# Differential attention: half of the weights-times-values products in split fp32r, and three quarters of the joining of the two maps on GpSimd

## The chip, the cores and the metric

The kernel runs on one core of one Trainium2 chip, in one launch. The metric is the device time in microseconds. Three runs of the kernel before took 2998.64, 2998.72 and 3003.08 us, median 2998.72. The profile shown here is of one further execution.

## The reference, cut to what matters

A two-layer encoder is applied to a prompt of 2048 tokens and a sample of 256 tokens with shared weights. The first layer mixes by differential attention, the second by a Fourier transform. The attention, per head (8 heads, two query/key maps of 64, values of 128):

```python
def block(start):
    qb = lax.dynamic_slice_in_dim(q, start, Q_BLOCK, axis=3)          # 128 queries, both maps
    s = jnp.einsum('bhmqd,bhmkd->bhmqk', qb, k, preferred_element_type=f32) * scale
    s = s - (slopes[:, None, None] * dist)[None, :, None]             # ALiBi
    p = jax.nn.softmax(s, axis=-1)
    pd = p[:, :, 0] - lam * p[:, :, 1]                                # the two maps are joined
    return jnp.einsum('bhqk,bhkv->bhqv', pd.astype(v.dtype), v)       # weights times values
```

Everything is float32.

## The kernel before, in words

The function `attend` does all heads in one program without a loop on the chip. A head has 17 steps: step q from 0 to 15 handles the scores of the q-th block of 128 prompt queries, and step 16 those of the sample. The work on one block is spread over several steps. In the terms of the code:

- **Scores.** Step q computes four halves (`score_half`, j = 0 to 3: map 0 keys 0 to 1023, map 0 keys 1024 to 2047, then map 1), each into one of three PSUM buffers of 1024 columns (`score`, RING = 3). VectorE takes the row maximum of each half (`maximum`, L1296) and scales it (`negative`, L1302). ScalarE takes the exponential of each half (`exponential`, L1220) with its row sums. A half can be written only when the exponential three halves earlier is done.
- **Joining.** In the next step VectorE adds the row sums and inverts them (`inverse_sums`, L1320, L1323; this runs behind the step's first row maximum), and p0/sum0 - lambda * p1/sum1 is formed in place: GpSimd scales the first half of map 1 (L1388, 1024 keys), then the second half of map 1 (L1391) and of map 0 (L1393), and adds these two (L1396). VectorE does the first half of the keys with one scalar_tensor_tensor (`combine`, L1334), the last thing in its step.
- **Turning.** One step later, TensorE transposes the joined block in four units of four key blocks (`turn_weights`, c = 0 to 3, L1096) into one single PSUM buffer `turned` of 512 columns; ScalarE copies each unit to SBUF (`take_weights`, L1198). The next unit must wait for that copy. In steps 1 to 5 a unit of the values is transposed too (`turn_value`, L1105, copied by `take_v`, L1204, which stands between the third and the fourth exponential on ScalarE).
- **Products.** `pair_product` (L1122, and L1116 for the sample) multiplies 16 key blocks by a pair of query blocks, 256 columns, into `o_acc`. The table `QUARTERS` deals 130 products to the quarters of the steps; in steps 5 to 14 each quarter has two.

All five engines run in the order in which their code is written. TensorE's order in a usual step is: half 0, half 1, turn 0, pair 0, turn 1, half 2, pair 1, turn 2, half 3, turn 3, pair 2, turn_value (steps 1 to 5), pair 3. VectorE's is: maximum 0, inverse_sums, maximum 1, negative 0, maximum 2, maximum 3, negative 1, combine. In the profile one fp32 product or fp32 matmul of the program shows as two MATMUL records, an fp32r one as one.

## Time and profile before

| | us |
|---|---|
| median of three runs | 2998.72 |
| the profiled execution | 3001.8 |
| its span, first to last instruction | 2999.7 |
| TensorE busy in the span | 2834.2 (94%) |
| VectorE | 1831.8 (61%) |
| ScalarE | 1740.7 (58%) |
| GpSimd | 1637.9 (55%) |
| attention stage, about 852 to 2081 | 1229 |

The time of a run is some 2 us more than the span. Matmul durations in the timeline include their pipeline, so the pitch of matmuls is read from the difference of their starts.

### The profile page before, as it was taken

The numbers are of one execution on the slowest core, as the hardware profiler recorded it, in microseconds if no ns is written. First come the engines' busy times: TensorE is split into PE (matmuls) and PEld (weight loads), VectorE is DVE, ScalarE is ACT, GpSimd is POOL, SyncE is SP. The second block draws the span as 40 slices with busy tenths as digits, with TensorE's granted clock in tenths as the row PEclk, the third lists the DMA queues.
The fourth block names the chain that finished last, engine by engine and source line by source line (L and its number), as shares of the span: only waits on it lengthen the run. The fifth ranks groups of instructions, "written<-read, shape, count | busy, mean of one in ns | idle before, by whom it ended". The sixth has DMA issues, their size and how long they took to land. (4 is left out here: it accounts for less than half of the span.)

```text
span 2999.7 us, 41691 instructions
## 1 busy us (share of the span) xinstructions
PE 2834.2 (94%) x15098; PEld 2493.8 (83%) x15098; DVE 1831.8 (61%) x2402; ACT 1740.7 (58%) x3126; POOL 1637.9 (55%) x1060
## 2 busy tenths in 40 slices
PE   3899999999899999999999999998999899899898
PEld 3899999999778787878888888886688899887687
DVE  7668767866476777777777777776886200441322
ACT  4777766776477777777777777775443321322321
POOL 5888764654266566656665666665664320230642
PEclk8999999999999999999999999999999999999899
DMA  2654464356344413141313232121565522555752
GB/s 84 197 173 166 146 198 127 118 181 201 101 130 138 107 34 102 35 108 36 98 46 76 65 74 64 37 90 60 199 207 172 187 90 77 158 168 186 263 186 102
DMA packets 281816, 374.03 MB, mean 125 GB/s; under 512 B 22923, under 2 KB 258507, under 8 KB 276140
## 3 DMA queue, kind: packets, MB, share of 16 engines
q1 hardware_dynamic: 279404, 369.14, 39.6%
q8 instruction: 121, 1.98, 0.3%
q10 hardware_dynamic: 2080, 2.10, 0.2%
q14 instruction: 83, 0.68, 0.1%
q0 software_dynamic: 128, 0.13, 0.0%
HBM read 258.04 MB, written 125.97 MB: 128 GB/s over the span
## 5 line engine op out<-in xcount | busy, mean ns | idle before, releaser
L1296 DVE TENSOR_REDUCE pa_half_max<-pa_score 128x1 f32<-128x1024 f32 x512 | 624.2, 1219 | 324.9 <-PE pa_score L1066 324.4
L1220 ACT ACTIVATE pa_p<-pa_score,pa_neg_max 128x1024 f32<-128x1024 f32 x512 | 567.7, 1111 | 68.6 <-DVE pa_neg_max L1302 68.4
L206 PE MATMUL ia_acc<-ia_xh,ia_wh 128*128 128x384 f32 x1344 | 459.9, 342 | 73.3 <-DVE ia_xl L686 44.1
L1122 PE MATMUL pa_o_acc<-pa_wt,pa_vv 128*128 128x256 f32 x2048 | 514.0, 380 | 1.5 <-ACT pa_o_out_s L1259 1.5
L1062 PE MATMUL pa_score<-pa_ka,pa_qa 128*128 128x512 f32 x1024 | 454.9, 444 | 13.2 <-ACT pa_p L1220 6.6
L207 PE MATMUL ia_acc<-ia_xl,ia_wh 128*128 128x384 f32 x1344 | 456.2, 339 | 0.0
L208 PE MATMUL ia_acc<-ia_xh,ia_wl 128*128 128x384 f32 x1344 | 455.8, 339 | 0.0
L1198 ACT ACTIVATE pa_wt<-pa_turned 128x512 f32<-128x512 f32 x512 | 306.3, 598 | 241.4 <-PE pa_turned L1096 236.4
L443 POOL TENSOR_TENSOR ia_w_sums<-ia_raw 128x512 f32<-128x512 f32 x240 | 334.3, 1401 | 174.3 <-PE ia_acc L208 158.8
L1066 PE MATMUL pa_score<-pa_kb,pa_qb 96*128 96x512 f32 x1024 | 422.9, 413 | 0.0
L1122 PEld LDWEIGHTS pa_o_acc<-pa_wt,pa_vv 128*128 128x128 f32 x2048 | 366.2, 190 | 44.8 <-ACT pa_o_out_s L1259 3.2
L1388 POOL TENSOR_SCALAR pa_p<-pa_p,pa_inv_sum,pa_lam_neg 128x1024 f32<-128x1024 f32 x128 | 153.6, 1200 | 447.8 <-DVE pa_inv_sum L1323 447.8
L206 PEld LDWEIGHTS ia_acc<-ia_xh,ia_wh 128*128 128x128 f32 x1344 | 258.2, 192 | 79.8 <-issue 79.4
L1096 PE MATMUL pa_turned<-pa_ident,pa_p 128*128 128x128 f32 x2048 | 313.0, 275 | 3.9 <-ACT pa_wt L1198 3.6
L1396 POOL TENSOR_TENSOR pa_p<-pa_p 128x1024 f32<-128x1024 f32 x128 | 302.4, 2363 | 23.8 <-POOL pa_p L1393 23.8
L1096 PEld LDWEIGHTS pa_turned<-pa_ident,pa_p 128*128 128x128 f32 x2048 | 243.1, 140 | 77.8 <-ACT pa_wt L1198 39.5
L670 DVE TENSOR_TENSOR ia_wl<-ia_acc,ia_wh 128x512 fp32r<-128x512 f32 x336 | 227.1, 683 | 84.4 <-ACT ia_acc L569 83.3
L706 DVE TENSOR_TENSOR ia_c<-ia_c,ia_acc 128x384 f32<-128x384 f32 x384 | 198.3, 547 | 126.2 <-PE ia_acc L208 116.6
L207 PEld LDWEIGHTS ia_acc<-ia_xl,ia_wh 128*128 128x128 f32 x1344 | 258.3, 192 | 0.5
L208 PEld LDWEIGHTS ia_acc<-ia_xh,ia_wl 128*128 128x128 f32 x1344 | 257.8, 192 | 0.0
L1062 PEld LDWEIGHTS pa_score<-pa_ka,pa_qa 128*128 128x128 f32 x1024 | 196.4, 192 | 53.1 <-ACT pa_p L1220 13.7
L1066 PEld LDWEIGHTS pa_score<-pa_kb,pa_qb 96*128 96x128 f32 x1024 | 196.9, 192 | 33.6
...
## 6 DMA issues: line engine op xcount, KB each, us to landing
...
```

The source lines that it names most:

```text
L206: pe.matmul(out, a_hi(k), b_hi(k), start=first and n == 0, stop=False)
L207: pe.matmul(out, a_hi(k), b_lo(k), start=False, stop=False)
L208: mm = pe.matmul(out, a_lo(k), b_hi(k), start=False, stop=last and n == len(ks) - 1)
L443: pool.tensor_tensor(w_sums[:, s % RING], x, y, op).then_inc(w_sum, 1)
L1062: pe.matmul(out[:, c], qa[s][:, n, at:at + P], ka[hs][:, n, cols], start=True, stop=False)
L1066: mm = pe.matmul(out[:, c], qb[s][:, n, at:at + P], kb[hs][n][:, cols], start=False, stop=True)
L1096: mm = pe.transpose(turned[:, x * P:(x + 1) * P], src, ident[:])
L1122: mm = pe.matmul(acc, vv[:, k], wt[:, g % 2, k], start=k == 0, stop=k == NB - 1)
L1198: act.activation(wt[:, s, 4 * c:4 * c + 4, at:at + P], turned[:].rearrange("p (k t) -> p k t", k=4), ACT.Copy).then_inc(turned_out, 1)
L1220: act.activation(dst[:, half * HALF:(half + 1) * HALF], score[:, (4 * q + j) % RING].rearrange("p a b -> p (a b)"), ACT.Exp, bias=neg_max[ ...
L1296: dve.tensor_reduce(half_max[:, q % 2, n, half:half + 1], score[:, (4 * q + j) % RING].rearrange("p a b -> p (a b)"), AX_X, ALU.max).then_ ...
L1396: pool.tensor_tensor(b, b, p1[:, par, HALF:], ALU.add).then_inc(weights_rest, 1)
```

## The change

Key blocks 4 to 7 and 12 to 15 (units c = 1 and 3, `LOW`) are kept as two fp32r numbers, a rounded one and the remainder, for the weights (`wt_hi`, `wt_lo`) and the values (`vv_hi`, `vv_lo`). Their product is three fp32r matmuls of 256 columns in place of one fp32 one. ScalarE's copy writes the rounded part; VectorE writes the remainder, PSUM minus rounded part (`weights_low`, L1379 of the changed kernel, and `v_low`, L1385), after which `turned` may be overwritten: every turn waits for the semaphore `low_out` as well. `weights_low` for c = 1 stands between negative 0 and maximum 2; for c = 3 it stands behind combine, and `v_low` behind that (steps 2 and 4). On TensorE `turn_value` moves behind pair 3. GpSimd's part of the joining grows from 1024 to 1536 of 2048 keys, and VectorE's combine shrinks from 1024 to 512; turn 1 waits for GpSimd's part, before it was turn 2, and the third exponential does, before the fourth. To make room, some small tiles share memory and the sample uses the diagonal table of the last pair (one DMA a head less).

```diff
@@ attend: buffers @@
+    LOW = (1, 3)
+    LOW_NB = 4 * len(LOW)
...
-        vv = m.sb("vv", [P, NB + 2, P])
+        vv = m.sb("vv", [P, NB + 2 - LOW_NB, P])
+        vv_hi = m.sb("vv_hi", [P, LOW_NB, P], F32R)
+        vv_lo = m.sb("vv_lo", [P, LOW_NB, P], F32R)
...
-        wt = m.sb("wt", [P, 2, NB, PAIR])
+        wt = m.sb("wt", [P, 2, NB - LOW_NB, PAIR])
+        wt_hi = m.sb("wt_hi", [P, 2, LOW_NB, PAIR], F32R)
+        wt_lo = m.sb("wt_lo", [P, 2, LOW_NB, PAIR], F32R)
...
@@ TensorE: turn_weights, turn_v, pair_product, step @@
-                    if c == 2:
+                    if c == 1:
                         pe.wait_ge(weights_rest, NB * h + t - 1 if t >= 2 else NB * h)
                     wait(pe, turned_out, unit(h, t, "w", c))
+                    wait(pe, low_out, lows(h, t, "w", c))
...
                     wait(pe, turned_out, unit(h, t, "v", c))
+                    wait(pe, low_out, lows(h, t, "v", c))
...
+                                if c in LOW:
+                                    pe.wait_ge(low_out, lows(h, t, kind, c) + 1 - (LOWS if late else 0))
+                            if is_low(k):
+                                at = low_at(k)
+                                pe.matmul(acc, vv_hi[:, at], wt_hi[:, g % 2, at], start=False, stop=False)
+                                pe.matmul(acc, vv_hi[:, at], wt_lo[:, g % 2, at], start=False, stop=False)
+                                mm = pe.matmul(acc, vv_lo[:, at], wt_hi[:, g % 2, at], start=False, stop=k == NB - 1)
...
                         pair(2)
+                        pair(3)
                         turn_value(q - 1)
-                        pair(3)
@@ ScalarE: take_weights, take_v, exponential @@
+                    dst = wt_hi[:, s, low_at(4 * c):low_at(4 * c) + 4, at:at + P] if c in LOW else \
+                        wt[:, s, full_at(4 * c):full_at(4 * c) + 4, at:at + P]
...
-                    if j == 3 and not (is_first(h) and q < 2):
+                    if j == 2 and not (is_first(h) and q < 2):
                         act.wait_ge(weights_rest, NB * h + (q - 1 if q >= 1 else -1))
@@ VectorE: combine, new weights_low and v_low, step @@
-                    a, par = p0[:, (q - 1) % 4, :HALF], (q - 1) % 2
-                    dve.scalar_tensor_tensor(out=a, in0=a, scalar=inv_sum[:, par, 0:1], in1=p1[:, par, :HALF],
+                    a, par = p0[:, (q - 1) % 4, :GROUP], (q - 1) % 2
+                    dve.scalar_tensor_tensor(out=a, in0=a, scalar=inv_sum[:, par, 0:1], in1=p1[:, par, :GROUP],
                                              op0=ALU.mult, op1=ALU.add).then_inc(weights, 1)
+
+                def weights_low(h, t, c):
+                    dve.wait_ge(turned_out, unit(h, t, "w", c) + 1)
...
+                    dve.tensor_tensor(wt_lo[:, s, ks, at:at + P], turned[:].rearrange("p (k t) -> p k t", k=4),
+                                      f32(wt_hi[:, s, ks, at:at + P]), ALU.subtract).then_inc(low_out, 1)
...
                             negative(h, q, 0)
+                        low(1)
+                        if parts["score"]:
                             maximum(h, q, 2)
                             maximum(h, q, 3)
                             negative(h, q, 1)
                     if parts["before"]:
                         combine(h, q)
+                    low(3)
+                    if parts["score"] and (q, "v", q - 1) in place and q - 1 in LOW:
+                        v_low(h, q, q - 1)
@@ GpSimd @@
-                    pool.tensor_scalar(p1[:, par, :HALF], p1[:, par, :HALF], inv_sum[:, par, 1:2], lam["neg"][:, 0:1],
+                    pool.tensor_scalar(p1[:, par, :GROUP], p1[:, par, :GROUP], inv_sum[:, par, 1:2], lam["neg"][:, 0:1],
                                        ALU.mult, ALU.mult).then_inc(p1_scaled, 1)
-                    b = p0[:, (q - 1) % 4, HALF:]
+                    b = p0[:, (q - 1) % 4, GROUP:]
...
-                    pool.tensor_tensor(b, b, p1[:, par, HALF:], ALU.add).then_inc(weights_rest, 1)
+                    pool.tensor_tensor(b, b, p1[:, par, GROUP:], ALU.add).then_inc(weights_rest, 1)

```

How VectorE's order changes, first before. From the reciprocal of one step to that of the next (pa_half_max: a row maximum; pa_p: the combine):

```order
L1320 TENSOR_TENSOR pa_row_sum<-pa_half_sum 128x2
L1323 RECIPROCAL pa_inv_sum<-pa_row_sum 128x2
L1296 TENSOR_REDUCE pa_half_max<-pa_score 128x1
L1302 TENSOR_SCALAR pa_neg_max<-pa_half_max 128x1
L1296 TENSOR_REDUCE pa_half_max<-pa_score 128x1 x2
L1302 TENSOR_SCALAR pa_neg_max<-pa_half_max 128x1
L1334 SCALAR_TENSOR_TENSOR pa_p<-pa_p,pa_inv_sum 128x1024
L1296 TENSOR_REDUCE pa_half_max<-pa_score 128x1
```

and now, in step 4 of a head:

```order
L1357 TENSOR_TENSOR pa_row_sum<-pa_half_sum 128x2
L1360 RECIPROCAL pa_inv_sum<-pa_row_sum 128x2
L1333 TENSOR_REDUCE pa_half_max<-pa_score 128x1
L1339 TENSOR_SCALAR pa_neg_max<-pa_half_max 128x1
L1379 TENSOR_TENSOR pa_wt_lo<-pa_turned,pa_wt_hi 128x4x128
L1333 TENSOR_REDUCE pa_half_max<-pa_score 128x1 x2
L1339 TENSOR_SCALAR pa_neg_max<-pa_half_max 128x1
L1371 SCALAR_TENSOR_TENSOR pa_p<-pa_p,pa_inv_sum 128x512
L1379 TENSOR_TENSOR pa_wt_lo<-pa_turned,pa_wt_hi 128x4x128
L1385 TENSOR_TENSOR pa_vv_lo<-pa_turned,pa_vv_hi 128x512
L1333 TENSOR_REDUCE pa_half_max<-pa_score 128x1
```

Two remainders of the weights and one of the values have come in, two of the three directly behind the combine and ahead of the next step's first row maximum.

TensorE at the end of step 4, before (L1096 is turn 3, L1105 turn_value, L1062 the first matmul of step 5):

```order
L1096 MATMUL pa_turned<-pa_ident,pa_p 128x128 x4
L1122 MATMUL pa_o_acc<-pa_wt,pa_vv 128x256
L1105 MATMUL pa_turned<-pa_ident,pa_vt 128x128 x4
L1122 MATMUL pa_o_acc<-pa_wt,pa_vv 128x256
L1062 MATMUL pa_score<-pa_ka,pa_qa_51 128x512
```

and now (L1123, L1133 and L1088 in their place):

```order
L1123 MATMUL pa_turned<-pa_ident,pa_p 128x128 x4
L1154 MATMUL pa_o_acc<-pa_wt_hi,pa_vv_hi 128x256
L1155 MATMUL pa_o_acc<-pa_wt_lo,pa_vv_hi 128x256
L1156 MATMUL pa_o_acc<-pa_wt_hi,pa_vv_lo 128x256
L1154 MATMUL pa_o_acc<-pa_wt_hi,pa_vv_hi 128x256
L1155 MATMUL pa_o_acc<-pa_wt_lo,pa_vv_hi 128x256
L1156 MATMUL pa_o_acc<-pa_wt_hi,pa_vv_lo 128x256
L1133 MATMUL pa_turned<-pa_ident,pa_vt 128x128 x4
L1088 MATMUL pa_score<-pa_ka,pa_qa_51 128x512
```

Each of the two products has become three matmuls, and the values are turned behind both. 

GpSimd keeps its order of four instructions a step; three of them, two TENSOR_SCALAR and the TENSOR_TENSOR, have 1536 columns where they had 1024, and the first TENSOR_SCALAR 512.

## Rows read from the trace of the kernel before

**Rows 1.** Windows: stretch, length, busy us of each engine (instructions), clock, DMA.

```profile
852.00:2081.00 1229.00, 1211.10 (x6583) 1007.39 (x6582) 887.42 (x1181) 909.03 (x1680) 764.65 (x519) 1.00 0.26 73
1401.70:1410.90 9.20, 9.20 (x52) 7.76 (x51) 6.77 (x10) 6.78 (x13) 5.92 (x4) 1.00 0.02 5
```

**Rows 2.** Waits inside the attention stage: us in total, times, longest.

```profile
PEld pa_turned L1096 <- ACT pa_wt L1198: 37.6, 173, 1.0
PEld pa_turned L1105 <- ACT pa_wt L1198: 24.2, 30, 1.1
```

**Rows 3.** Timeline of TensorE, one step: start us, us, what, count.

```profile
1403.86 0.60 PE L1096 MATMUL pa_turned<-pa_ident,pa_p 128*128 128x128 f32 x4
1404.30 1.03 PE L1122 MATMUL pa_o_acc<-pa_wt,pa_vv 128*128 128x256 f32 x4
1405.16 0.64 PE L1096 MATMUL pa_turned<-pa_ident,pa_p 128*128 128x128 f32 x4
...
1409.37 1.89 PE L1122 MATMUL pa_o_acc<-pa_wt,pa_vv 128*128 128x256 f32 x8
1410.91 0.58 PE L1062 MATMUL pa_score<-pa_ka,pa_qa 128*128 128x512 f32 x1
```

**Rows 4.** TensorE timeline, fp32r products of 260 columns, Fourier layer.

```profile
2576.26 0.28 PE L207 MATMUL fl_ps<-fl_wc,fl_ring 128*128 128x260 f32 x1
...
2577.94 0.28 PE L206 MATMUL fl_ps<-fl_wc,fl_ring 128*128 128x260 f32 x1
```

**Rows 5.** Timeline of ScalarE, same step as rows 3.

```profile
1404.50 0.60 ACT L1198 ACTIVATE pa_wt<-pa_turned 128x512 f32<-128x512 f32 x1 [0.75 <-PE pa_turned L1096]
```

**Rows 6.** Timeline of VectorE, same step.

```profile
1404.35 0.17 DVE L1323 RECIPROCAL pa_inv_sum<-pa_row_sum 128x2 f32<-128x2 f32 x1
...
1410.53 1.40 DVE L1334 SCALAR_TENSOR_TENSOR pa_p<-pa_p,pa_inv_sum 128x1024 f32<-128x1024 f32 x1
1412.23 1.22 DVE L1296 TENSOR_REDUCE pa_half_max<-pa_score 128x1 f32<-128x1024 f32 x1 [0.30 <-PE pa_score L1066]
```

**Rows 7.** Timeline of GpSimd, same step.

```profile
1404.73 1.21 POOL L1388 TENSOR_SCALAR pa_p<-pa_p,pa_inv_sum,pa_lam_neg 128x1024 f32<-128x1024 f32 x1 [3.09 <-DVE pa_inv_sum L1323]
...
1408.48 2.36 POOL L1396 TENSOR_TENSOR pa_p<-pa_p 128x1024 f32<-128x1024 f32 x1 [0.18 <-POOL pa_p L1393]
```

**Rows 8.** Timeline of GpSimd, a step with a long overlap.

```profile
1452.97 2.36 POOL L1396 TENSOR_TENSOR pa_p<-pa_p 128x1024 f32<-128x1024 f32 x1 [0.18 <-POOL pa_p L1393]
```

**Rows 9.** Timeline of VectorE, that step.

```profile
1454.31 2.10 DVE L1334 SCALAR_TENSOR_TENSOR pa_p<-pa_p,pa_inv_sum 128x1024 f32<-128x1024 f32 x1
```

**Rows 10.** Line 1334, all executions: ns shortest/median/longest.

```profile
L1334 DVE SCALAR_TENSOR_TENSOR pa_p<-pa_p,pa_inv_sum x128: 1275/1391/2956, 831.5 to 2057.3; 128x1024 f32<-128x1024 f32 x128
```

**Rows 11.** Groups of GpSimd: busy us, mean ns of one.

```profile
L1388 POOL TENSOR_SCALAR pa_p<-pa_p,pa_inv_sum,pa_lam_neg 128x1024 f32<-128x1024 f32 x128 | 153.6, 1200 | 447.8 <-DVE pa_inv_sum L1323 447.8
...
L2005 POOL TENSOR_TENSOR fg_xl<-fg_h_in,fg_xh 128x1536 fp32r<-128x1536 f32 x10 | 35.1, 3515 | 108.0 <-ACT fg_xh L2038 108.0
...
L1383 POOL TENSOR_SCALAR pa_p_s<-pa_p_s,pa_inv_s,pa_lam_neg 128x256 f32<-128x256 f32 x16 | 8.8, 559 | 4.7 <-DVE pa_inv_s L1316 4.7
```

**Rows 12.** Groups of VectorE: a difference of PSUM and SBUF; the row maximum.

```profile
L1296 DVE TENSOR_REDUCE pa_half_max<-pa_score 128x1 f32<-128x1024 f32 x512 | 624.2, 1219 | 324.9 <-PE pa_score L1066 324.4
L670 DVE TENSOR_TENSOR ia_wl<-ia_acc,ia_wh 128x512 fp32r<-128x512 f32 x336 | 227.1, 683 | 84.4 <-ACT ia_acc L569 83.3
```

**Rows 13.** Timeline of VectorE, reciprocals of steps 1 and 6.

```profile
1448.85 0.17 DVE L1323 RECIPROCAL pa_inv_sum<-pa_row_sum 128x2 f32<-128x2 f32 x1
...
1495.65 0.17 DVE L1323 RECIPROCAL pa_inv_sum<-pa_row_sum 128x2 f32<-128x2 f32 x1
```

**Rows 14.** Line 1316, once a head: first and last start.

```profile
L1316 DVE RECIPROCAL pa_inv_s<-pa_sum_s x8: 166/168/178, 972.0 to 2061.3; 128x4 f32<-128x4 f32 x8
```

**Rows 15.** Windows around an idle stretch of TensorE, columns as in rows 1.

```profile
2114.80:2117.40 2.60, 0.03 (x1) 0.00 (x1) 2.56 (x3) 1.06 (x1) 1.12 (x1) 1.00 0.09 32
2117.50:2121.00 3.50, 3.50 (x5) 1.47 (x6) 3.50 (x2) 1.07 (x2) 2.27 (x2) 0.53 0.00 0
```

More of the change, by code:

```diff
@@ L835, in attend @@
         qb_s = m.sb("qb_s", [HD + ALIBI, 2, SHORT], F32R)
-        diag_s = m.sb("diag_s", [P, P], F32R)
+        p_s_at = (nc.sbuf_base + 31) // 32 * 32
         p_s = m.sb("p_s", [P, 2, 2, SHORT])
-        wt_s = m.sb("wt_s", [P, 2, SHORT])
+        wt_s = p_s[:, 1]
         o_out_s = m.sb("o_out_s", [P, SHORT])
@@ L845, in attend @@
         ones = m.sb("ones", [P, P])
-        sq = m.sb("sq", [P, 2, 2, GROUP])
-        row_w = m.sb("row_w", [P, 1])
-        eps = m.sb("eps", [P, 1])
+        small = m.sb("small", [P, 3])
+        row_w, eps = small[:, 0:1], small[:, 1:2]
         score = m.ps("score", [P, RING, 2, GROUP])
@@ L878, in attend @@
         pool_held, sp_held = m.sem("pool_held"), m.sem("sp_held")
-        lam = load_lambda(m, m.sem("lam_in"))
+        lam = load_lambda(m, m.sem("lam_in"), p_s_at, small[:, 2:3])
         order = []
@@ L892, in unit, with lows, is_low, full_at @@
             return UNITS * h + place[(t, kind, c)] - SKIPPED
+        low_order = [x for x in order if x[2] in LOW]
+        LOWS = len(low_order)
+        SKIPPED_LOWS = len(LOW)
+        def lows(h, t, kind, c):
+            return LOWS * h + sum(place[x] < place[(t, kind, c)] for x in low_order) - SKIPPED_LOWS
+        def is_low(k):
+            return k // 4 in LOW
+        def full_at(k):
+            return sum(not is_low(x) for x in range(k))
+        def low_at(k):
+            return sum(is_low(x) for x in range(k))
         def turned_block(t):
@@ L979, in load_sample @@
                         sp.dma_start(f32(qb_s[HD:, n]), row(consts["penalty"], h, 0, ALIBI, 0, SHORT)).then_inc(sample_in, 16)
-                    sp.dma_start(f32(diag_s[:]), row(consts["diag"], h, 0, P, 0, P)).then_inc(sample_in, 16)
                 def load_v(h):
@@ L1078, in score_sample @@
                         pe.matmul(out, qa_s[:, n, at], ka_s[:, n], start=True, stop=False)
-                        pe.matmul(out[:, at], ident_r[:], diag_s[:], start=False, stop=False)
+                        pe.matmul(out[:, at], ident_r[:], diag[1][:], start=False, stop=False)
                         mm = pe.matmul(out, qb_s[:, n, at], kb_s[:, n], start=False, stop=True)
@@ L1115, in pair_product @@
                                 pe.wait_ge(turned_out, unit(h, 1, "w", 0) + 1)
-                            mm = pe.matmul(acc, vv[:, NB + k], wt_s[:, k], start=k == 0, stop=k == 1)
+                            mm = pe.matmul(acc, vv[:, full_at(NB + k)], wt_s[:, k], start=k == 0, stop=k == 1)
                         else:
@@ L1121, in pair_product @@
                                 pe.wait_ge(turned_out, unit(h, t, kind, c) + 1 - (UNITS if late else 0))
-                            mm = pe.matmul(acc, vv[:, k], wt[:, g % 2, k], start=k == 0, stop=k == NB - 1)
+                                if c in LOW:
[5 more added lines that the diff above has]
+                                mm = pe.matmul(acc, vv_lo[:, at], wt_hi[:, g % 2, at], start=False, stop=k == NB - 1)
+                            else:
+                                mm = pe.matmul(acc, vv[:, full_at(k)], wt[:, g % 2, full_at(k)], start=k == 0, stop=False)
                         if k == (1 if g == NP else NB - 1):
@@ L1203, in take_v @@
                     n = 4 if c < NC else 2
-                    act.activation(vv[:, 4 * c:4 * c + n], turned[:, :n * P].rearrange("p (k t) -> p k t", k=n),
-                                   ACT.Copy).then_inc(turned_out, 1)
+                    dst = vv_hi[:, low_at(4 * c):low_at(4 * c) + n] if c in LOW else vv[:, full_at(4 * c):full_at(4 * c) + n]
+                    act.activation(dst, turned[:, :n * P].rearrange("p (k t) -> p k t", k=n), ACT.Copy).then_inc(turned_out, 1)
                 def exponential(h, q, j):
@@ L1332, in combine, with v_low, low @@
                         return
-                    a, par = p0[:, (q - 1) % 4, :HALF], (q - 1) % 2
-                    dve.scalar_tensor_tensor(out=a, in0=a, scalar=inv_sum[:, par, 0:1], in1=p1[:, par, :HALF],
+                    a, par = p0[:, (q - 1) % 4, :GROUP], (q - 1) % 2
+                    dve.scalar_tensor_tensor(out=a, in0=a, scalar=inv_sum[:, par, 0:1], in1=p1[:, par, :GROUP],
                                              op0=ALU.mult, op1=ALU.add).then_inc(weights, 1)
+                def weights_low(h, t, c):
+                    dve.wait_ge(turned_out, unit(h, t, "w", c) + 1)
+                    b = turned_block(t)
+                    s, at = (b // 2) % 2, (b % 2) * P
+                    ks = slice(low_at(4 * c), low_at(4 * c) + 4)
+                    dve.tensor_tensor(wt_lo[:, s, ks, at:at + P], turned[:].rearrange("p (k t) -> p k t", k=4),
+                                      f32(wt_hi[:, s, ks, at:at + P]), ALU.subtract).then_inc(low_out, 1)
+                def v_low(h, t, c):
+                    dve.wait_ge(turned_out, unit(h, t, "v", c) + 1)
+                    ks = slice(low_at(4 * c), low_at(4 * c) + 4)
+                    dve.tensor_tensor(vv_lo[:, ks], turned[:].rearrange("p (k t) -> p k t", k=4),
+                                      f32(vv_hi[:, ks]), ALU.subtract).then_inc(low_out, 1)
                 def step(h, hs, q):
                     parts = step_parts(h, q)
+                    def low(c):
+                        if parts["weights"] and (q, "w", c) in place:
+                            weights_low(h, q, c)
                     if q == SAMPLE:
@@ L1350, in step @@
                             negative(h, q, 0)
+                        low(1)
+                        if parts["score"]:
                             maximum(h, q, 2)
```

22 lines of the change are left out of this document (13 added, 9 removed).

## The prediction

> **What bounds the kernel now.** I read first the windows: the attention stage takes 1229 us, TensorE is busy in 1211.1 of them at full clock (1.00), and in one usual step for all of its 9.20 us, where VectorE has 6.77, ScalarE 6.78 and GpSimd 5.92 [rows 1]. So TensorE's work is the step, if nobody keeps it waiting. Second, the waits: its weight loads wait for ScalarE's copy of `turned` 173 times (37.6 us) and in front of the value turns 30 times (24.2 us) [rows 2]. These are the places where a copy is just in time. Third, the timelines of one step side by side: TensorE [rows 3], ScalarE [rows 5], VectorE [rows 6] and GpSimd [rows 7]. Fourth, how long the combine (L1334) lasts when GpSimd works beside it [rows 8 to 10]. The last is what decides here.
>
> **TensorE's saving.** Four records of an old product take 1405.16 - 1404.30 = 0.86 us [rows 3]; they are two products, so one is 0.43. An fp32r matmul of 260 columns follows another at (2577.94 - 2576.26)/14 = 0.120 us (14 steps between these starts) [rows 4], so three take 0.36. A split product saves 0.07 us. By `QUARTERS` 64 of a head's 128 are split: 64 x 8 x 0.07 = 36 us at best. The first quarter keeps nothing. There turn 1 starts at 1405.16, and ScalarE's copy of turn 0 ends at 1404.50 + 0.60 = 1405.10 [rows 3, 5]: a shorter pair 0 only waits for it. Steps 5 to 15 have 22 split products there. That leaves 42 x 8 x 0.07 = 24 us, if the rest of the step follows. Bounds for the three fp32r matmuls: 0.36, or with a format change at either side some 0.45, which would make this nothing.
>
> **VectorE's work.** A remainder is a TENSOR_TENSOR of 512 columns out of PSUM and SBUF. The same form is L670: 0.683 us, 336 times [rows 12]. Two a step add 1.37 us. The combine falls from 1024 to 512 columns: its shortest is 1.275 us [rows 10], less 512 columns at some 1.04 ns is 0.74, so 0.53 us less. Its sum, 6.77 + 0.84 = 7.6 us, would fit in 9.2. ScalarE's copies keep their size; I cost the other destination at nothing.
>
> **GpSimd's chain.** Let R be the end of the reciprocal, 1404.52 in the step shown [rows 6]. GpSimd starts at R + 0.21 (1404.73) and starts its TENSOR_TENSOR at R + 3.96, ending at R + 6.32 (1410.84) [rows 7]. TENSOR_SCALAR takes 0.559 us for 256 columns and 1.200 for 1024 [rows 11], so 0.77 for 512 and 1.63 for 1536. A TENSOR_TENSOR of 1536 takes 3.515 [rows 11]. New chain: 0.21 + 0.77 + 1.63 + 1.63 + 0.18 (the old pause) less 0.04 of overlaps, so the TENSOR_TENSOR starts at R + 4.4 and ends at R + 7.9. If the scalings grew in proportion to the columns (1.8 each) it would end at R + 8.2. Alone this fits: turn 1 needs it 1.5 us later than that in an undelayed step, and 7.9 is under 9.
>
> **The combine meets GpSimd.** This is the step that turns the sum. The combine of rows 9 starts at 1454.31 and ends at 1456.41. GpSimd's TENSOR_TENSOR ends at 1455.33 [rows 8]; the difference is 1.08 us. In the step of rows 6 and 7 the combine ends at 1411.93, 1.09 behind 1410.84. Before, this cost little, since the combine comes at R + 6.0 (1410.53) and GpSimd ends at R + 6.3. Now GpSimd ends at R + 7.9.
>
> The Trainium skill ("SBUF — State Buffer", section "SBUF: two separate sides") has this as a rule: VectorE and GpSimd share a port pair under an exclusive lock, held for the whole instruction, and a VectorE instruction with two SBUF inputs counts, which the combine has. By that rule the combine of the changed kernel ends at R + 8.45; were the port shared by bandwidth, it would end about R + 7.3. The rows of this case bear out the lock, and I forecast by them.
>
> **The new loop.** Behind the combine VectorE now has the remainder of unit 3, then the next step's first maximum, row sums and reciprocal; that starts GpSimd again. Can the combine come before GpSimd's TENSOR_TENSOR at R + 4.4? VectorE must first do maximum, negative, remainder, two maxima and negative: 1.20 + 0.21 + 0.68 + 1.22 + 1.22 + 0.21 = 4.7 us behind R. With TensorE's order (turn 0 released with the remainder of unit 3, half 3 behind it) I get R + 5.3. Too late by either, so it waits each time. The loop is then: 7.9 (GpSimd) + 0.55 (combine) + 0.68 (remainder, rows 12) + 1.22 (maximum, rows 12) + 0.35 (row sums and reciprocal) less 0.3 of overlaps = 10.4 us, from reciprocal to reciprocal. TensorE has 8.9 us of work in it and waits some 1.4 us before turn 0, for the remainder that frees `turned`. The step goes from 9.2 to 10.4.
>
> **The sum for a head.** A head lasts (2061.3 - 972.0)/7 = 155.6 us now [rows 14].
> - Steps 6 to 15, nine intervals of 9.22: each +1.2, so +10.6.
> - Steps 1 to 6, now 1495.65 - 1448.85 = 46.8 us [rows 13]. In steps 2 to 5 the value turn waits for the remainder of unit 3, ScalarE's copy of it follows, the fourth exponential stands behind that copy, and the next row sums need it; in steps 2 and 4 `v_low` (0.68) comes too, before the next maximum. Behind the combine's end at R + 8.45 I count: remainder 0.6, turn 0.6, copy 0.6, `v_low` 0.7, maximum 1.2, row sums and reciprocal 0.3: 12.4 us for steps 2 and 4, 12.1 for 3, 11.9 for 5, and 9.8 for 1, which has no remainder. Sum 58.6, so +11.8.
> - Step 15 over the sample step and step 0 to step 1: no large GpSimd work meets a combine in step 0. TensorE bounds; the delays and the saving give +0.4.
>
> +22.8 a head, +182 us for eight.
> - The clock. In steps 2 to 5 TensorE idles 3 to 5 us before the value turn. Idle for 2.60 us at 2114.8, it went on at 0.53 of the clock, that is at the lower of the two levels (1.2 and 2.4 GHz) for nearly all of the 3.5 us behind it [rows 15]. A turn and one half at half speed are 1.4 us more on the path. 32 such places, at half of that price: +20 us, with bounds of 0 and 45. The waits of 1.4 us in a usual step I cost at none.
>
> Sum: the profiled execution's 3001.8 + 202 = 3204, and against the median of 2998.7 some 3200 us. The removed DMA and the moved tiles are nothing in this.
>
> **Rivals.**
> - *TensorE's saving comes through.* VectorE had 2.4 us free in the step [rows 1], and all fits if the combine isn't held: 2998.7 - 24 = 2975 us. For it: the saving is real. Against it: the two ends 1.08 us behind GpSimd. It needs all of the value turns' waits hidden as well. 0.04.
> - *No lock loop, but the single `turned` buffer.* Say the combine ends at R + 6.8 whatever GpSimd does. Then usual steps keep the saving, but the value turns wait for the remainder of unit 3 in steps 2 to 5: 1.4 + 1.7 + 1.4 + 1.0 = 5.5 us a head, 44 in all: 2998.7 - 24 + 44 = 3019. It decides from the point at which that remainder ends later than pair 3. 0.05.
> - *Every second combine slips in.* If VectorE reaches it before R + 4.4 after a late step, GpSimd waits instead, for 0.55 us, the next step is early, and its combine is held again. The mean step is (9.05 + 10.4)/2 = 9.7: some 9 us a head less than forecast, 3125. For it: the margin is 0.3 us against the bare sum of VectorE's work, 0.9 by TensorE's order. 0.07.
> - *The clock falls in usual steps also.* Waits of 1.4 us in each step would then bring the lower level, and TensorE's 8.9 us of work no longer fit: at +1.6 us in 72 usual steps, 3315. Against it: nothing in rows 1 and 15 shows a fall behind so short a wait. 0.06.
>
> **How the numbers follow.** The forecast, held combines with a loop of 10.4, has 0.78. Its own range: 7.9 to 8.2 for GpSimd is up to +0.3 a step, +35 us; the value steps are good to 0.6 us each, 20 us in all; the clock 0 to 45. That is 3140 to 3260. Toward the slipping rival and the clock's I widen to 3110 to 3270, which leaves out the two small cases and most of the fourth. Faster by over 0.2% (what a measurement of this kernel can tell): 0.04. Within 0.2%: 0.01. Slower: 0.95.
>
> **What would show it.** Right: reciprocal to reciprocal 10.4 us in steps 6 to 15; the combine's mean near 3 us though it has half the columns, ending 0.55 behind GpSimd's TENSOR_TENSOR; VectorE's idle time small there; TensorE idle before turn 0, released by VectorE's L1379; the value turns waiting 3 us or more; the stage at some 1430 us; the clock in it below 1.00. Wrong: a combine of 0.75 us (no lock at this size), a combine that starts before the TENSOR_TENSOR (slipping), a remainder longer than 0.7 beside GpSimd (it would be held as well), or split products at over 0.45 us.

## The result, and the profile after

The changed kernel takes 3224.39 us (median of 4 executions, 3219.61 to 3226.48), the kernel before in the same session 2998.68. The ratio is 1.0748, with a 95% interval of 1.0729 to 1.0767: slower by 226 us. The forecast was 3200. The profiled execution has a span of 3224.7 us.

The windows of the changed kernel, cut at the stages' borders as in [rows 1], with the same columns, put nearly the whole loss into the attention stage:

```profile
0.00:852.00 852.00, 754.17 (x4132) 738.61 (x4132) 595.26 (x885) 558.23 (x1044) 536.51 (x398) 0.95 0.51 151
852.00:2305.00 1453.00, 1265.11 (x7141) 1049.48 (x7142) 1191.96 (x1459) 930.45 (x1696) 956.31 (x523) 0.96 0.23 63
2305.00:3224.00 919.00, 856.96 (x4339) 738.42 (x4337) 347.79 (x332) 264.86 (x387) 335.82 (x140) 0.97 0.50 167
```

From the border at 852 us on, the stage grows from 1229 to 1453 us, which is 224 of the 226. But 10 of these lie ahead of it: the first matmul of the stage starts at 805.07 us in the kernel before and at 814.99 in the changed one, so the changed kernel is 10 us behind when the window opens.

```profile
805.07 0.47 PE L1062 MATMUL pa_score<-pa_ka,pa_qa 128*128 128x512 f32 x1 [1.80 <-PEq L87]
```

```profile
814.99 0.47 PE L1088 MATMUL pa_score<-pa_ka,pa_qa 128*128 128x512 f32 x1 [1.79 <-PEq L87]
```

So attention itself costs 214 us, and the input stage, which has 4058 matmuls in both profiles, 10. Why it takes longer no run shows. Inside the windows TensorE was busy in all but 18 us and now idles for 188, and its clock is 0.96 on average instead of 1.00. (TensorE's busy time grows although it has less work, since part of it runs at the lower clock.)

The waits inside the stage, in us in total, times and longest, answer to [rows 2]:

```profile
PEld pa_turned L1123 <- DVE pa_p L1371: 107.0, 83, 1.5
PE pa_turned L1133 <- DVE pa_wt_lo L1379: 101.8, 32, 4.3
PE pa_turned L1123 <- DVE pa_wt_lo L1379: 80.2, 86, 2.2
```

L1123 and L1133 are now the turns and the value turns, L1371 is the combine and L1379 the remainder. Where ScalarE's copy was just in time before, VectorE is now late, and in all 32 value turns of steps 2 to 5 it is late by 3.2 us on average.

Two groups of the changed kernel (busy us, mean ns of one), for [rows 8 and 10]. The combine of half as many columns takes 1.8 times as long as the old one, whose mean was 1.476 us (2.95 to 2.99 us in usual steps, less in steps 2 to 5, where VectorE comes to it later):

```profile
L1457 POOL TENSOR_TENSOR pa_p<-pa_p 128x1536 f32<-128x1536 f32 x128 | 446.8, 3490 | 23.8 <-POOL pa_p L1454 23.8
...
L1371 DVE SCALAR_TENSOR_TENSOR pa_p<-pa_p,pa_inv_sum 128x512 f32<-128x512 f32 x128 | 336.1, 2626 | 0.0
```

VectorE's timeline in a usual step, from one reciprocal to the next (start us, us, what), for [rows 6]:

```profile
1476.82 0.17 DVE L1360 RECIPROCAL pa_inv_sum<-pa_row_sum 128x2 f32<-128x2 f32 x1
...
1482.43 2.99 DVE L1371 SCALAR_TENSOR_TENSOR pa_p<-pa_p,pa_inv_sum 128x512 f32<-128x512 f32 x1
1485.35 0.68 DVE L1379 TENSOR_TENSOR pa_wt_lo<-pa_turned,pa_wt_hi 128x512 fp32r<-128x512 f32 x1
1485.95 1.21 DVE L1333 TENSOR_REDUCE pa_half_max<-pa_score 128x1 f32<-128x1024 f32 x1
1487.08 0.14 DVE L1357 TENSOR_TENSOR pa_row_sum<-pa_half_sum 128x2 f32<-128x2 f32 x1
1487.26 0.17 DVE L1360 RECIPROCAL pa_inv_sum<-pa_row_sum 128x2 f32<-128x2 f32 x1
```

GpSimd's timeline in the same step, for [rows 7]:

```profile
1477.20 0.77 POOL L1449 TENSOR_SCALAR pa_p<-pa_p,pa_inv_sum,pa_small 128x512 f32<-128x512 f32 x1 [2.76 <-DVE pa_inv_sum L1360]
1477.95 1.63 POOL L1452 TENSOR_SCALAR pa_p<-pa_p,pa_inv_sum,pa_small 128x1536 f32<-128x1536 f32 x1
1479.55 1.64 POOL L1454 TENSOR_SCALAR pa_p<-pa_p,pa_inv_sum,pa_ones 128x1536 f32<-128x1536 f32 x1
1481.38 3.50 POOL L1457 TENSOR_TENSOR pa_p<-pa_p 128x1536 f32<-128x1536 f32 x1 [0.18 <-POOL pa_p L1454]
```

Read the two together. With R = 1476.99, the end of the reciprocal, GpSimd's last instruction runs from R + 4.39 to R + 7.89. The combine starts inside it, at R + 5.44, and ends at R + 8.43, 0.54 us behind it. Remainder, maximum, row sums and reciprocal follow without a gap, and the reciprocal comes 10.44 us after the one before. This is no single case: of the stage's 128 combines 119 begin inside GpSimd's addition, and all of these end 0.54 to 0.56 us behind it.

Eight of the other nine are those of step 16, one a head. They come ahead of the addition and fall into GpSimd's scaling of map 0 (L1454) instead:

```profile
1552.38 2.01 DVE L1371 SCALAR_TENSOR_TENSOR pa_p<-pa_p,pa_inv_sum 128x512 f32<-128x512 f32 x1
```

```profile
1552.22 1.63 POOL L1454 TENSOR_SCALAR pa_p<-pa_p,pa_inv_sum,pa_ones 128x1536 f32<-128x1536 f32 x1
1554.03 3.69 POOL L1457 TENSOR_TENSOR pa_p<-pa_p 128x1536 f32<-128x1536 f32 x1 [0.18 <-POOL pa_p L1454]
```

The scaling ends at 1553.85 and the combine at 1554.39, 0.54 behind it. So not the addition alone holds a combine. The addition then starts while the combine still runs and takes 3.69 us instead of 3.50.

Value steps are longer still. TensorE, ScalarE and VectorE at one value turn, in step 3 of the fourth head (one fence for each engine):

```profile
1416.44 0.63 PE L1133 MATMUL pa_turned<-pa_ident,pa_vt 128*128 128x128 f32 x4 [3.39 <-DVE pa_wt_lo L1379]
...
1418.22 0.63 PE L1088 MATMUL pa_score<-pa_ka,pa_qa 128*128 128x512 f32 x1
```

```profile
1417.11 0.60 ACT L1242 ACTIVATE pa_vv<-pa_turned 128x512 f32<-128x512 f32 x1 [1.75 <-PE pa_turned L1133]
```

```profile
1415.62 0.68 DVE L1379 TENSOR_TENSOR pa_wt_lo<-pa_turned,pa_wt_hi 128x512 fp32r<-128x512 f32 x1
1418.46 1.23 DVE L1333 TENSOR_REDUCE pa_half_max<-pa_score 128x1 f32<-128x1024 f32 x1 [2.16 <-PE pa_score L1092]
```

TensorE stands 3.39 us for the remainder; the next maximum needs the half that TensorE does only behind that, so VectorE then waits 2.16 us for TensorE. A score matmul of 512 columns takes 0.63 us here instead of 0.40: the clock has fallen, as two windows around the value turn show (columns of [rows 1]):

```profile
1413.00:1416.40 3.40, 0.05 (x1) 0.00 (x0) 3.26 (x4) 2.08 (x5) 2.15 (x1) 1.00 0.44 127
1416.45:1419.90 3.45, 3.45 (x13) 2.75 (x14) 1.41 (x3) 1.97 (x4) 0.00 (x0) 0.68 0.20 64
```

Idle for 3.4 us, TensorE goes on at 0.68 of the clock on average, that is at the lower level (1.2 GHz) for some two thirds of the second window.

The reciprocals of one head, start to start, give the whole picture. The intervals of each row are worked out from the starts in the fourth head (for the kernel before, [rows 13 and 14] have two of the intervals' sums). The time at the lower clock leaves out the first stretch of some 20 us, which every version has at the start of the stage, and what lies behind the last head's steps. "Stage from" is the start of the stage's first matmul:

| kernel | step 1 | steps 2 to 5 | usual step | last, sample to next step 1 | combine, mean us | us at the lower clock in the stage | stage from, us | median us |
|---|---|---|---|---|---|---|---|---|
| before | 8.8 | 9.2 to 9.8 | 9.2 | 8.82 + 17.25 | 1.476 | 0 | 805.1 | 2998.7 |
| changed | 9.84 | 13.07, 12.64, 12.53, 13.25 | 10.42 | 10.08 + 16.49 | 2.626 | 109 | 815.0 | 3224.4 |
| split only (1) | 8.80 | 12.67, 13.87, 12.82, 11.32 | 9.40 | 9.06 + 16.39 | 1.807 | 109 | 813.6 | 3114.0 |
| join only (2) | 9.81 | 9.79, 9.80, 9.80, 9.78 | 9.80 | 9.46 + 17.09 | 2.798 | 7 | 806.0 | 3060.1 |
| changed, remainder first (3) | 9.82 | 10.39, 9.79, 10.40, 9.80 | 9.82 | 9.49 + 18.19 | 2.365 | 17 | 815.4 | 3100.0 |
| changed, no addition (4) | 8.58 | 10.67, 10.44, 10.83, 11.62 | 9.20 | 8.96 + 17.04 | 0.795 | 44 | 809.6 | 3054.8 |
| split only, remainder first (5) | 8.80 | 9.77, 9.76, 10.12, 9.54 | 9.18 | 8.86 + 16.89 | 1.358 | 10 | 812.7 | 3022.3 |
| changed, addition in 3 pieces (6) | 8.80 | 10.46, 12.71, 12.81, 11.49 | 8.8 or 9.45 | 9.12 + 16.78 | 1.358 | 65 | 811.3 | 3095.1 |
| changed, TensorE kept busy (7) | 9.81 | 12.57, 12.38, 12.56, 12.16 | 10.41 | 10.09 + 16.54 | 2.788 | 7 | 809.5 | 3198.8 |
| one unit split, half join (8) | 8.81 | 9.50, 8.79, 9.48, 9.31 | 9.08 or 9.35 | 8.94 + 17.61 | 1.496 | 0 | 813.1 | 2997.6 |

The heads differ somewhat in steps 2 to 5, where the clock falls more often in some than in others. From the reciprocal of step 1 to that of step 6 the eight heads of the changed kernel take 61.2 to 64.3 us, 62.7 on average; the mean is 46.9 in the kernel before, 58.6 in (1), 49.1 in (2), 53.3 in (4), 48.9 in (5), 56.0 in (6) and 59.6 in (7).

### The profile page after: what moved, and what is told of

Read it like the earlier page. It is cut to its first block and busy times, and to the rows that moved or that the text cites. A ratio compares the mean times of both kernels' runs of the same rounds, so it can differ in the third digit from the quotient of the medians.

```text
span 3224.7 us, 43269 instructions
## 1 busy us (share of the span) xinstructions
PE 2876.2 (89%) x15610; PEld 2526.5 (78%) x15610; DVE 2135.0 (66%) x2674; ACT 1753.5 (54%) x3126; POOL 1828.6 (57%) x1060
## 5 line engine op out<-in xcount | busy, mean ns | idle before, releaser
L1257 ACT ACTIVATE pa_p<-pa_score,pa_neg_max 128x1024 f32<-128x1024 f32 x512 | 568.0, 1111 | 70.0 <-DVE pa_neg_max L1339 67.1
L1088 PE MATMUL pa_score<-pa_ka,pa_qa 128*128 128x512 f32 x1024 | 465.0, 454 | 11.9 <-ACT pa_p L1257 5.5
L1457 POOL TENSOR_TENSOR pa_p<-pa_p 128x1536 f32<-128x1536 f32 x128 | 446.8, 3490 | 23.8 <-POOL pa_p L1454 23.8
L1092 PE MATMUL pa_score<-pa_kb,pa_qb 96*128 96x512 f32 x1024 | 443.1, 433 | 0.0
L1123 PE MATMUL pa_turned<-pa_ident,pa_p 128*128 128x128 f32 x2048 | 318.4, 278 | 89.3 <-DVE pa_wt_lo L1379 80.6
L1123 PEld LDWEIGHTS pa_turned<-pa_ident,pa_p 128*128 128x128 f32 x2048 | 239.2, 142 | 182.3 <-DVE pa_p L1371 107.0
L1449 POOL TENSOR_SCALAR pa_p<-pa_p,pa_inv_sum,pa_small 128x512 f32<-128x512 f32 x128 | 98.9, 772 | 479.0 <-DVE pa_inv_sum L1360 479.0
L1371 DVE SCALAR_TENSOR_TENSOR pa_p<-pa_p,pa_inv_sum 128x512 f32<-128x512 f32 x128 | 336.1, 2626 | 0.0
L1236 ACT ACTIVATE pa_wt<-pa_turned 128x512 f32<-128x512 f32 x256 | 153.3, 599 | 294.5 <-PE pa_turned L1123 294.5
L1158 PE MATMUL pa_o_acc<-pa_wt,pa_vv 128*128 128x256 f32 x1024 | 263.8, 380 | 0.0
L1088 PEld LDWEIGHTS pa_score<-pa_ka,pa_qa 128*128 128x128 f32 x1024 | 208.5, 204 | 62.4 <-ACT pa_p L1257 33.4
L1092 PEld LDWEIGHTS pa_score<-pa_kb,pa_qb 96*128 96x128 f32 x1024 | 209.1, 204 | 35.2
```

Source lines behind the costliest of these rows:

```text
L1088: pe.matmul(out[:, c], qa[s][:, n, at:at + P], ka[hs][:, n, cols], start=True, stop=False)
L1092: mm = pe.matmul(out[:, c], qb[s][:, n, at:at + P], kb[hs][n][:, cols], start=False, stop=True)
L1123: mm = pe.transpose(turned[:, x * P:(x + 1) * P], src, ident[:])
L1158: mm = pe.matmul(acc, vv[:, full_at(k)], wt[:, g % 2, full_at(k)], start=k == 0, stop=False)
L1257: act.activation(dst[:, half * HALF:(half + 1) * HALF], score[:, (4 * q + j) % RING].rearrange("p a b -> p (a b)"), ACT.Exp, bias=neg_max[ ...
L1371: dve.scalar_tensor_tensor(out=a, in0=a, scalar=inv_sum[:, par, 0:1], in1=p1[:, par, :GROUP], op0=ALU.mult, op1=ALU.add).then_inc(weights, 1)
```

## Experiments

The numbers in brackets are those of the table. The kernel before was run beside each. Theory L is the forecast's: the combine is held by GpSimd's instruction. N is the rival with the single `turned` buffer and no hold; G says that VectorE waits for GpSimd's whole share; C is the clock.

**(1) Split only.** The products stay split, the joining goes back to half and half, and with it the two waits for GpSimd's part.

```diff
-a, par = p0[:, (q - 1) % 4, :GROUP], (q - 1) % 2
+a, par = p0[:, (q - 1) % 4, :HALF], (q - 1) % 2
...
-b = p0[:, (q - 1) % 4, GROUP:]
+b = p0[:, (q - 1) % 4, HALF:]
...
```

> The split products stay; the joining goes back to half and half (GpSimd's instructions 1024 columns, VectorE's combine 1024). Theory L (the combine is held until GpSimd's TENSOR_TENSOR ends, and the remainder of unit 3, the next maximum and the reciprocal follow it in a loop): GpSimd ends at R + 6.3, the combine at R + 7.4, the loop is 9.4 us where the change has 10.42; value steps lose as much; 16 us a head: 3098 us. Theory N (no hold; the new remainders on the single buffer turned make the time, whoever joins): VectorE has 0.5 us more, so 3225 or above.

Measured: 3114.04 us, ratio 1.0390 [1.0373, 1.0408], 16 us over the expected sum; theory N's 3225 is far off. The usual step is 9.40, as expected. Steps 1 to 5 lose 11.7 us a head over the kernel before, of the 15.8 that they lose with the whole change. So most of their length comes with the split products, whose remainder stands behind a combine that GpSimd's old share holds too (mean 1.807 us), and not with GpSimd's larger share.

**(2) Join only.** The kernel before, with three quarters joined by GpSimd and no split product; the edit is that of (1) read backwards, on the kernel before.

> No split products; only the joining moves (GpSimd three quarters, combine 512 columns). Theory L: the combine ends at R + 8.4, maximum and reciprocal follow: loop 9.8 us against 9.2, value steps 9.8 as well: +8 us a head, 3066 us. Theory N: VectorE has less to do and GpSimd fits in the step: 2999 us, no change.

Measured: 3060.10 us, ratio 1.0214 [1.0198, 1.0229], 6 us under the expected sum. Every step is 9.8 long, value steps too. VectorE's timeline of a usual step in (2):

```profile
1401.75 2.96 DVE L1334 SCALAR_TENSOR_TENSOR pa_p<-pa_p,pa_inv_sum 128x512 f32<-128x512 f32 x1
1404.63 1.21 DVE L1296 TENSOR_REDUCE pa_half_max<-pa_score 128x1 f32<-128x1024 f32 x1
```

The hold is there without any remainder. (1) and (2) alone cost 117 and 63 us over the kernel before, run beside them, together 180; the change costs 226. The missing 46 is for the most part the remainder behind a held combine. A usual step grows by 0.2 in (1), by 0.6 in (2) and by 1.2 with both, so 0.4 more than the two together, which is 29 us in 72 such steps; steps 1 to 5 grow by 1.8 us a head more than the two together, which is 15.

**(3) Remainder first.** In the changed kernel the remainder of unit 3 goes ahead of the combine.

```diff
+low(3)
 if parts["before"]:
     combine(h, q)
-low(3)
```

> The changed kernel, but VectorE makes the remainder of unit 3 ahead of the combine instead of behind it. Theory L: the remainder falls into the time in which the combine is held, and turned comes free at R + 6.2 instead of R + 9.0: loop 9.8 us, value steps 9.8 to 10.4 where they have 12.1 to 13.7, the clock falls no more: 18 us a head less, 3077 us. Theory N: the order of two instructions that both run back to back changes the loop by nothing and the value turn by 0.5 us: above 3200.

Measured: 3099.98 us, ratio 1.0344 [1.0329, 1.0359], 23 us over the expected sum. Usual steps came out as expected, and so did the value steps of the fourth head. 14 of the 23 us are in the sample step, where unit 3's turn comes last, so that the remainder made the combine behind it wait: 18.19 instead of 16.49, 8 times. Of the other 9, part is the clock, which was not to fall any more and was low for 17 us (in five heads steps 1 to 5 take 51 us or more, against 50.2 in the fourth); the rest I can't place. VectorE and GpSimd of (3) in a value step:

```profile
1353.17 0.68 DVE L1379 TENSOR_TENSOR pa_wt_lo<-pa_turned,pa_wt_hi 128x512 fp32r<-128x512 f32 x1
1353.77 2.42 DVE L1371 SCALAR_TENSOR_TENSOR pa_p<-pa_p,pa_inv_sum 128x512 f32<-128x512 f32 x1
1356.11 0.68 DVE L1385 TENSOR_TENSOR pa_vv_lo<-pa_turned,pa_vv_hi 128x512 fp32r<-128x512 f32 x1
```

```profile
1352.16 3.46 POOL L1457 TENSOR_TENSOR pa_p<-pa_p 128x1536 f32<-128x1536 f32 x1 [0.18 <-POOL pa_p L1454]
```

The remainder lies wholly inside GpSimd's instruction and takes its usual 0.68: with one operand in PSUM it isn't held (119 remainders of (3) begin inside the addition, and each takes 0.68 or 0.69). The combine, with both inputs in SBUF, is, until 0.57 us behind 1355.62. Moving the remainder costs nothing there and frees `turned` 3 us earlier.

**(4) No addition on GpSimd.** The changed kernel without GpSimd's TENSOR_TENSOR, so three quarters of the keys are left unjoined.

```diff
-pool.tensor_scalar(b, b, inv_sum[:, par, 0:1], ones[:, 0:1], ALU.mult, ALU.mult).then_inc(p0_rest, 1)
...
-pool.tensor_tensor(b, b, p1[:, par, GROUP:], ALU.add).then_inc(weights_rest, 1)
+pool.tensor_scalar(b, b, inv_sum[:, par, 0:1], ones[:, 0:1], ALU.mult, ALU.mult).then_inc(weights_rest, 1)
```

> The changed kernel without GpSimd's TENSOR_TENSOR (the two maps' last three quarters are not added; the computation is changed there). Theory L: nothing holds the combine, since GpSimd's last instruction ends at R + 4.2 before it: combine some 0.75 us, usual steps bound by TensorE at about 9.05 us, value turns still wait for the remainder of unit 3 at R + 6.8: 3019 us (2990 to 3040). Theory N: still near 3224.

Measured: 3054.75 us, ratio 1.0197 [1.0179, 1.0215], 36 us over the expected sum and outside its range (2990 to 3040), though far from theory N's 3224. The combine falls to its bare time, as one row of a usual step shows, the last below. The value steps lose 5.3 us over [rows 13] in the fourth head (8.58 + 10.67 + 10.44 + 10.83 + 11.62 = 52.1 against 46.8) and 6.4 on average, where the rival had worked out 5.5; the clock, low for 44 us, is in the measured ones. And the usual step is 9.20 and not 9.05: TensorE's saving doesn't come. ScalarE, TensorE and VectorE of (4) around half 1 of a usual step show why:

```profile
1411.32 1.11 ACT L1257 ACTIVATE pa_p<-pa_score,pa_neg_max 128x1024 f32<-128x1024 f32 x1 [0.38 <-DVE pa_neg_max L1339]
...
1412.33 0.19 ACT L1257 ACTIVATION_READ_ACCUMULATOR pa_p<-pa_score,pa_neg_max 128x1 f32 x1
```

```profile
1403.37 0.50 PE L1088 MATMUL pa_score<-pa_ka,pa_qa 128*128 128x512 f32 x1
...
1412.33 0.40 PE L1092 MATMUL pa_score<-pa_kb,pa_qb 96*128 96x512 f32 x1
...
1412.57 0.50 PE L1088 MATMUL pa_score<-pa_ka,pa_qa 128*128 128x512 f32 x1
...
1412.91 0.22 PE L1091 MATMUL pa_score<-pa_diag,pa_ident_r 128*128 128x128 f32 x1
```

```profile
1412.57 0.19 PEld L1088 LDWEIGHTS pa_score<-pa_ka,pa_qa 128*128 128x128 f32 x1 [0.29 <-ACT pa_p L1257]
```

```profile
1409.81 1.22 DVE L1333 TENSOR_REDUCE pa_half_max<-pa_score 128x1 f32<-128x1024 f32 x1 [0.84 <-PE pa_score L1092]
...
1411.20 0.74 DVE L1371 SCALAR_TENSOR_TENSOR pa_p<-pa_p,pa_inv_sum 128x512 f32<-128x512 f32 x1
```

The third exponential ends with the read of its accumulator, at 1412.52, and half 1 follows at 1412.57 with a matmul of 0.50 us instead of 0.40, and the next row of TensorE comes at 0.34 instead of 0.24: it was held by 0.1, and its weight load names the exponential (ACT, L1257) as what released it. The loop closes without a gap: from half 1 at 1403.37 to the maximum of half 3, at 1409.81, it is 6.44 us, and from there over negative, exponential and the accumulator's read to the next half 1 another 2.76, together the step's 9.20. TensorE's timeline shows the split pair itself as cheap as I had it:

```profile
1410.05 1.03 PE L1158 MATMUL pa_o_acc<-pa_wt,pa_vv 128*128 128x256 f32 x4
1410.73 0.47 PE L1154 MATMUL pa_o_acc<-pa_wt_hi,pa_vv_hi 128*128 128x256 f32 x1
...
1411.86 0.40 PE L1092 MATMUL pa_score<-pa_kb,pa_qb 96*128 96x512 f32 x1
```

From the full pair to the second score matmul it is 1411.86 - 1410.05 = 1.81 us. Four full products from 1409.37 [rows 3] to the same matmul, at 1411.33 in the kernel before, took 1.96. That is 0.15 for two split products, 0.07 each. Of the 0.15, 0.1 goes to the wait for the exponential, and pair 0 gives nothing, as forecast. The second split pair, at 1410.73, lies outside the loop above, so shortening it can't shorten the step.

**(5) Split only, remainder first.** (1), with the edit of (3) outside the sample step.

> Split products, joining half and half, and the remainder of unit 3 ahead of the combine (behind it in the sample step). Theory L: GpSimd ends at R + 6.3, the combine at R + 7.4, the next maximum follows at once: that loop is 8.8 us, under TensorE's 9.2, so usual steps are as before the change. Value turns wait only for maximum 3, negative 1 and the remainder: 0.66 us less than without GpSimd's addition, so +2.9 us a head against the kernel before: 3020 us. If single buffering by itself costs more than that, 3050.

Measured: 3022.29 us, ratio 1.0081 [1.0064, 1.0098]. The usual step is back at 9.18. Of the 24 us that are left, 16 are in steps 1 to 5 (48.9 against 46.9 us a head) and come with the wait for the remainder in front of the value turns; the later start of the stage (812.7 against 805.1) is the other 8. The waits of (5) in the stage:

```profile
PE pa_turned L1133 <- DVE pa_wt_lo L1379: 33.1, 31, 1.8
```

**(6) Addition in three pieces.** The changed kernel; GpSimd adds 3 x 512 columns.

```diff
-pool.tensor_tensor(b, b, p1[:, par, GROUP:], ALU.add).then_inc(weights_rest, 1)
+for x in range(3):
+    c = pool.tensor_tensor(b[:, x * GROUP:(x + 1) * GROUP], b[:, x * GROUP:(x + 1) * GROUP],
+                           p1[:, par, (x + 1) * GROUP:(x + 2) * GROUP], ALU.add)
+c.then_inc(weights_rest, 1)
```

> The changed kernel with GpSimd's TENSOR_TENSOR of 1536 columns cut into three of 512: the same work, 0.3 to 0.4 us longer in all. Theory L says that the hold lasts for an instruction: the combine gets in behind the first or second piece, ends at R + 6.2 or 7.5, and usual steps take 9.2 to 9.5 us: 3075 us (3050 to 3110). Theory G (the combine or the step waits for GpSimd's whole share of the joining, not for an instruction): GpSimd's end is later, the loop is 10.7 us, 3250 us.

Measured: 3095.07 us, ratio 1.0322 [1.0299, 1.0345], inside the expected range. This is the sharpest of the runs on the hold, since the same additions are made on the same data. G had 3250. A step of (6), GpSimd and VectorE, and the three pieces by line (ns shortest/median/longest, first and last start):

```profile
1437.44 4.22 POOL L1458 TENSOR_TENSOR pa_p<-pa_p 128x512 f32<-128x512 f32 x3 [0.18 <-POOL pa_p L1454]
```

```profile
1438.94 1.57 DVE L1371 SCALAR_TENSOR_TENSOR pa_p<-pa_p,pa_inv_sum 128x512 f32<-128x512 f32 x1
```

```profile
L1458 POOL TENSOR_TENSOR pa_p<-pa_p x3: 1272/1284/1747, 1437.4 to 1439.9; 128x512 f32<-128x512 f32 x3
```

The second piece runs from about 1438.7 to 1439.96. The combine comes at 1438.94 and ends at 1440.51, 0.55 behind that piece: it waits for one piece, not for all. The third piece then takes 1.747 us instead of 1.28, so GpSimd waits for VectorE in its turn. Usual steps are 8.8 or 9.45. Of the 97 us over the kernel before, some 73 are in steps 1 to 5 (56.0 against 46.9 us a head).

**(7) TensorE kept busy.** The changed kernel with 12 idle fp32r matmuls of 512 columns ahead of each value turn of steps 2 to 5.

```diff
+if 2 <= q <= NC + 1 and parts["score"]:
+    wait(pe, exps, SCORES * h + 4 * (q + 1) - RING + 1)
+    for x in range(12):
+        pe.matmul(score[:, (4 * (q + 1)) % RING, x % 2], ident_r[:], ka[hs][:, 0, :GROUP], start=True, stop=True)
 turn_value(q - 1)
```

> The changed kernel with 12 fp32r matmuls of 512 columns put ahead of the value turn in steps 2 to 5, where TensorE idles 2.3 to 4.9 us; they write a score buffer that is free and is overwritten by the next half. Theory C (part of the value steps' length is the lower clock behind the idle time): the clock stays at 1.00 in the stage, value steps take 12.4, 12.1, 12.4 and 11.9 us where they have 12.1 to 13.7: 32 us less, 3192 us. If the length is the chain of copies alone, 3225 or a little above.

Measured: 3198.75 us, ratio 1.0672 [1.0651, 1.0692]: 26 us less than the changed kernel, for more work (32 were expected). The windows of (7) at a value turn, as for the changed kernel above:

```profile
1396.60:1400.60 4.00, 3.06 (x12) 2.17 (x12) 3.90 (x4) 1.72 (x4) 2.78 (x1) 1.00 0.48 147
1400.70:1404.00 3.30, 3.30 (x19) 2.86 (x20) 1.56 (x4) 2.19 (x5) 0.00 (x0) 1.00 0.06 17
```

With 3.06 us of matmuls in the gap the clock stays at 1.00, and 19 matmuls fit where 13 did. The value turn has still waited 0.95 us for the remainder, so the twelve matmuls didn't hold it up. These 26 us are the clock's share; from the first to the last matmul of attention the two profiles differ by 24.

**(8) One unit split, half join.** `LOW = (1,)`: half as many split products, and no remainder of unit 3.

```diff
-LOW = (1, 3)
+LOW = (1,)
...
-low(3)
```

> Only unit 1 (key blocks 4 to 7) in split products, joining half and half; nothing of unit 3 stands behind the combine. Theory L: the loop is 8.8 us and TensorE bounds at 9.2; value turns wait for ScalarE's copies only: 2990 to 3000 us, the only form of the change that costs nothing. If the remainder of unit 1 between negative 0 and maximum 2 costs something by itself, 3010 or more.

Measured: 2997.62 us, ratio 0.9998 [0.9989, 1.0007]. Without the remainder of unit 3 the loss is gone. This version keeps the moved tiles, the dropped DMA and the new place of the value turn, so these cost little. The 32 split products a head that are left, 18 us by the forecast's 0.07, bring only a part of that. By the sample's reciprocals a head takes (2064.0 - 980.4)/7 = 154.8 us instead of 155.6, 6 us for eight, and the stage starts 8 us later (813.1 against 805.1), which takes them away again:

```profile
L1353 DVE RECIPROCAL pa_inv_s<-pa_sum_s x8: 166/169/177, 980.4 to 2064.0; 128x4 f32<-128x4 f32 x8
```

Of the versions tried none is faster than the kernel before.

## Why the prediction was right, and where it was off

- **The hold.** Right. The combine at R + 5.44 (5.3 forecast), its end at R + 8.43 (8.45), 0.54 behind GpSimd's instruction (0.55). (2), (4) and (6) show that GpSimd's instructions do it, here its TENSOR_TENSOR: the combine's mean is 2.80 with it, 0.795 without it, 1.36 with it in pieces. (The mean of the changed kernel is 2.63, where "near 3" was forecast; that holds in usual steps.) The section "SBUF: two separate sides" of the Trainium skill's page "SBUF — State Buffer" says that VectorE and GpSimd get their shared port pair as an exclusive lock for a whole instruction, not as a share of the bandwidth, and these rows agree: a combine waits for one instruction to end. The forecast's "about R + 7.3" for a shared bandwidth has no working behind it; twice the bare 0.74 from R + 5.3 on would be R + 6.8. Either is far from the 8.43 measured.
- **GpSimd's chain.** Right to 0.01: start at R + 4.39 (4.4), end at R + 7.89 (7.9).
- **The loop.** Right: 10.42 (10.4). (2) has the same sum without the remainder, 9.80. TensorE waits 1.06 us before turn 0, where 1.4 was forecast.
- **Slipping.** It didn't happen: in all usual steps the combine came behind the start of GpSimd's addition, but for one near the end of the eighth head. 5.44 against 4.39 is a margin of 1.05, near the 0.9 that the forecast had by TensorE's order.
- **Value steps.** The mechanism was right and the term too small. With the clock held up, in (7), the five intervals sum to 9.81 + 12.57 + 12.38 + 12.56 + 12.16 = 59.5 us against 58.6. From the combine's end to the next reciprocal's I had counted 4.0 us; in step 4 it is 4.14, from 1428.35 (1427.12 + 1.23) to 1432.49. The forecast's +11.8 a head is +12.7.

```profile
1427.12 1.23 DVE L1371 SCALAR_TENSOR_TENSOR pa_p<-pa_p,pa_inv_sum 128x512 f32<-128x512 f32 x1
...
1432.32 0.17 DVE L1360 RECIPROCAL pa_inv_sum<-pa_row_sum 128x2 f32<-128x2 f32 x1
```

- **The clock.** +20 forecast, +26 by (7), inside the bounds of 0 to 45. No usual step of the fourth head was touched, although TensorE waits 1.06 us in each: the rival by which the clock falls there too is refuted by 10.42 a step.
- **The rest.** +0.4 a head forecast; (10.08 + 16.49) - (8.82 + 17.25) = +0.5.
- **The sum.** A head by these: nine usual steps 10.8, value steps 12.7, rest 0.5, clock 26/8 = 3.2, together 27.2, or 218 for eight, against 202 forecast and 226 measured. The sample's reciprocals agree: a head takes (2288.3 - 1007.6)/7 = 183.0 us, 27.4 more than before.

```profile
L1353 DVE RECIPROCAL pa_inv_s<-pa_sum_s x8: 165/167/170, 1007.6 to 2288.3; 128x4 f32<-128x4 f32 x8
```

Of the 24 us that the forecast was short, 7 are the value steps' term, 6 the clock, 3 usual and other steps. The last 8 are mostly no part of a head. The input stage, which the forecast left as it was, takes 10 us more, with a cause that no run shows; the first and the last head, which I took to be like the others, cost some 4 less than 27.4 each, together; some 2 more lie elsewhere.

- **TensorE's saving.** The step that failed, though the forecast didn't rest on it. The forecast of the rivals counted 24 us off whenever VectorE wasn't late; (4) shows a usual step of 9.20, and (8) a head shorter by 0.8 us where 18/8 = 2.2 would have come. The size was right (0.07 a product), its effect wasn't: I had taken TensorE's busy 9.20 of 9.20 us as the step's only limit. The loop of half 3, maximum, negative, exponential 2 and half 1 is a second one, with the accumulator's read (0.19 us), which I left out, and it closes at 9.20 in (4), as long as TensorE's work was. So the rival's 3019 would have been about 3043, and (4) had 3055 with 44 us at the lower clock and a stage that starts 4.5 us later. That this loop is the limit is read from the held weight load of (4) and from the sum; no run shortened it, so it isn't shown by experiment.
